# Expert stage: scores of a choice between the sums of v, and at most four gathers in flight

## The chip, the core and the metric

The kernel runs on one core of a Trainium2 chip, as one program. The metric is the device time of one execution in microseconds. Three runs of the kernel before took 4378.47 us in the median (4372.89 to 4390.06). A further execution was taken by the hardware profiler; all rows below are of that one.

## The reference, cut to what matters

The network has two blocks; the first has two layers, each with a product-key expert part, `_peer`. For a token, eight heads each choose 16 of 16384 experts; an expert is one row of `u` and one row of `v`, of 1024 numbers each.

```python
def _peer(h, wq, keys, u, v):
    """PEER: 8 product-key retrieval heads over N_KEYS^2 single-neuron experts. h (B,S,D)."""
    ...
    def block(hb):
        tc = hb.shape[0]
        q = (hb @ wq).reshape(tc, PEER_HEADS, 2, PEER_HALF)
        s = jnp.einsum('thpk,hpnk->thpn', q, keys)
        s_top, i_top = lax.top_k(s, PEER_TOPK)
        cand = s_top[:, :, 0, :, None] + s_top[:, :, 1, None, :]
        cid = i_top[:, :, 0, :, None] * N_KEYS + i_top[:, :, 1, None, :]
        best, pos = lax.top_k(cand.reshape(tc, PEER_HEADS, -1), PEER_TOPK)
        eid = jnp.take_along_axis(cid.reshape(tc, PEER_HEADS, -1), pos, -1)
        g = jax.nn.softmax(best.astype(jnp.float32), -1).astype(hb.dtype)
        act = jax.nn.gelu(jnp.einsum('td,thed->the', hb, u[eid]), approximate=False)
        return jnp.einsum('the,thed->td', g * act, v[eid])
```

The first layer does this for 512 tokens (256 of the context, 256 of the sequence), the second for 256. Everything is float32.

## The kernel before, in words

The program is a chain of stages with a barrier between them. The change is in `stage_peer`, which runs twice: `l0_peer_experts` with four tiles of 128 tokens and `l1_peer_experts` with two. A step is one tile and one head: 32 steps in the first run, 16 in the second. Within a run the engines work as a pipeline over steps, and each engine has its own fixed program:

- TensorE (`pe`): `score(step)` multiplies the queries with the keys (L1195). Then, for each of the 16 experts of the step before (`step = b - 1`), it multiplies the gathered rows of `v` with a diagonal matrix of weights and adds them into the PSUM tile `acc` (L1217); that is called the sum of v here. A sum posts the semaphore `added`.
- VectorE (`dve`): for each expert of step `b` the dot product of the gathered row of `u` with the token (L1361), which posts `dotted`. After dot k of step b comes piece k of `pick(b + 2, k)`, the choice of the experts two steps on: piece 0 (L1270) waits for the scores, the pieces are linked by the semaphore `chain`, and the last one (L1326) writes the indices and posts `chosen`. `weigh` (L1342) makes the weights of the step before after dot 1.
- ScalarE (`act`): softmax exponentials (L1227), the gelu of the 16 dot products (L1249), and the 16 diagonal matrices (L1241).
- GpSimd (`pool`): one indirect DMA for each expert of `u` (L1182) and of `v` (L1187). Each gathers 128 rows of 4 KB, 0.52 MB. The rows of `u` land in eight slots of the weight buffer, those of `v` in eight slots of `ring`, and each slot has a semaphore of its own, `landed[...]`. In step b the gathers alternate: u of (b, k), then v of (b - 1, k). A gather of u waits for the dot that frees its slot (`dotted`, eight experts back), a gather of v for the sum that frees its slot (`added`, eight experts back). Nothing else limits how many are under way.

The order on each engine is the order in which this code is written; there is no scheduler. A score for step b + 2 stands in TensorE's order ahead of all 16 sums of step b - 1, and behind all sums of step b - 2.

Of the kernel before, what the change touches and what calls it, by code (L numbers as in the profile page):

```python
# [52 lines left out]
@contextmanager  # L53
def stage(nc, name):

    with ExitStack() as ctx:
        st = Stage(nc, name, ctx)
        yield st
        for s in st.sems:
            nc.gpsimd.sem_clear(s)  # L60
        nc.all_engine_barrier()
# [1060 lines left out]
HEADS, TOPK, KEYS = 8, 16, 128  # L1122
# [4 lines left out]
def stage_peer(nc, name, h, n_tiles, q_t, k_t, u, v, iota, ident, layer, y, diag, slots, landed, landed0):  # L1127

    RING = TOPK // 2
    with stage(nc, name) as st:
        v_ring = st.sb("ring", [P, RING, D])
        u_ring = slots.rearrange("p s k n -> p (s k n)").rearrange("p (s d) -> p s d", d=D)
# [24 lines left out]
        dotted, added, scored, chosen, h_ready, gelu_done, soft_in, soft_out, w_ready, diag_ready, sum_taken, chain = (  # L1159
            st.sem(n) for n in names)  # L1160
        steps = n_tiles * HEADS

        def landing(step, k):

            return landed0 + 16 * (2 * step + k // RING + 1)

# [3 lines left out]
        with nc.Block() as block:  # L1170
            @block.gpsimd
            def _(pool):
                for b in range(steps + 1):
                    if b < steps:

                        pool.wait_ge(chosen, b + 1)
                    for k in range(TOPK):
                        if b < steps:
                            if b * TOPK + k >= RING:

                                pool.wait_ge(dotted, b * TOPK + k - RING + 1)
                            pool.indirect_dma_start(u_ring[:, k % RING, :], None, u, bass.IndirectOffsetOnAxis(ap=picks[:, b % 4, k:k + 1], axis=0)).then_inc(landed[k % RING], 16)  # L1182
                        if b:
                            if (b - 1) * TOPK + k >= RING:

                                pool.wait_ge(added, (b - 1) * TOPK + k - RING + 1)
                            pool.indirect_dma_start(v_ring[:, k % RING, :], None, v, bass.IndirectOffsetOnAxis(ap=picks[:, (b - 1) % 4, k:k + 1], axis=0)).then_inc(landed[RING + k % RING], 16)  # L1187

            @block.tensor
            def _(pe):  # L1190
                def score(step):

                    t, head = divmod(step, HEADS)
                    for i in range(2):
                        last = nc.tensor.matmul(sc[:, step % 2, i, :], q_t[:, t, 2 * head + i, :], k_t[:, 2 * head + i, :], start=True, stop=True)  # L1195
                    last.then_inc(scored, 1)

                score(0)
                score(1)
                for b in range(steps + 1):  # L1200
                    if b + 2 < steps:

                        pe.wait_ge(chosen, b + 1)
                        score(b + 2)
                    if not b:
                        continue
                    step = b - 1
                    t, head = divmod(step, HEADS)
                    if head == 0 and t:

                        pe.wait_ge(sum_taken, t)
                    for k in range(TOPK):

                        pe.wait_ge(landed[RING + k % RING], landing(step, k))
                        pe.wait_ge(diag_ready, step * TOPK + k + 1)
                        for c in range(2):
                            last = nc.tensor.matmul(acc[:, c * BANK:(c + 1) * BANK], diag[:, step % 2 * TOPK + k, :], v_ring[:, k % RING, c * BANK:(c + 1) * BANK],  # L1217
                                                    start=(head == 0 and k == 0), stop=(head == HEADS - 1 and k == TOPK - 1))
                        last.then_inc(added, 1)
# [966 lines left out]
def peer(nc, weights, name, layer, n_tiles, consts, a, keys_t, h, h_t, y, landed, landed0):  # L2186

    with ExitStack() as ctx:
        sb = buffers(nc, ctx)
        q_t = sb(f"{name}_q_t", [P, n_tiles, HALVES, P])  # L2190
        stage_linear(nc, f"{name}_q", weights, h_t, token_tiles(n_tiles), q_t, feature=True)
        stage_peer(nc, f"{name}_experts", h, n_tiles, q_t[:, :, :, :], keys_t[:, :, :], a["peer_u"].rearrange("l e d -> (l e) d"),
                   a["peer_v"].rearrange("l e d -> (l e) d"), consts["iota"][:, :], consts["ident"][:, :], layer, y,
                   h_t[:, :, :].rearrange("p c (i t) -> p (c i) t", t=P), weights.slots[:, :, :, :], landed, landed0)
# [245 lines left out]
```

## Time and profile before

| what | value |
|---|---|
| median of three runs | 4378.47 us |
| profiled execution | 4386.04 us, its span 4384.2 us |
| busy: PE, DVE, POOL, ACT | 3239.2, 1863.4, 1443.9, 694.2 us |
| gathers: u, v | 768 and 768, 0.94 us of POOL each |
| data moved by the software queue | 805.40 MB of 1028.15 MB |

Read it so. The engines' busy times are of the whole span; the expert stages are the stretches from 785 to 2275 us and from 2795 to 3541 us, in which the line of the DMA is at 9 and the rate above 350 GB/s. POOL works there only. A row of the timeline has the start, the duration, the engine, the line and the tiles, and in brackets how long the engine sat idle before it and what ended that. "remote" and "issue" name no releaser of this program, and a wait that ended with many semaphore updates at once can be put down to any of them.

### The profile page before, as it was taken

The page shows a single profiled execution, that of the slowest core. Times are in us where ns is not written, and L with a number is a line of the kernel's source. Part 1 is how long each engine was busy: PE and PEld are TensorE (multiplying, and loading weights), DVE is VectorE, ACT ScalarE, POOL GpSimd, SP SyncE. Part 2 cuts the span into 40 slices and gives each one's busy share as a digit, 9 for nine tenths or more (in the row PEclk, how much of TensorE's full clock was granted, in tenths as well). Part 3 has the DMA queues.
Part 4 walks back from the last instruction along what each step waited for, and adds up shares of the span by engine and source line. Part 5 has one row for each costly group of instructions (what it writes and reads, how often), then busy time and mean ns, then how long its engine had stood idle before and what let it go on. Part 6 is the DMA issues. An engine that isn't in the chain of part 4 may idle for free. (4 is left out here: it accounts for less than half of the span.)

```text
span 4384.2 us, 28129 instructions
## 1 busy us (share of the span) xinstructions
PE 3239.2 (74%) x8452; PEld 1526.8 (35%) x8452; DVE 1863.4 (43%) x4661; ACT 694.2 (16%) x1660; POOL 1443.9 (33%) x1540
## 2 busy tenths in 40 slices
PE   6888769476767676776766886577677768888888
PEld 2343334222322232222223343422222234634573
DVE  1024630755556565555533073565556423232200
ACT  0012310111211111112110121112112113021100
POOL 0000000566666666666640000366666610000000
PEclk8987879799888898988888887788888989998999
DMA  4123221799989999999981233599999954332333
GB/s 170 66 80 113 80 86 38 295 366 351 375 350 357 364 362 354 371 361 359 370 323 63 79 116 115 212 359 366 355 354 372 362 195 144 112 115 99 115 132 125
DMA packets 355218, 1028.15 MB, mean 235 GB/s; under 512 B 53492, under 2 KB 58100, under 8 KB 355060
## 3 DMA queue, kind: packets, MB, share of 16 engines
q0 software_dynamic: 221184, 805.40, 47.8%
q1 hardware_dynamic: 131824, 217.57, 14.6%
q10 hardware_dynamic: 2068, 3.47, 0.3%
q8 instruction: 66, 1.08, 0.1%
q14 instruction: 76, 0.62, 0.0%
HBM read 1025.19 MB, written 1.15 MB: 234 GB/s over the span
## 5 line engine op out<-in xcount | busy, mean ns | idle before, releaser
L1217 PE MATMUL l_peer_experts_acc<-l_peer_experts_ring,h_t 128*128 128x512 f32 x3072 | 1541.5, 649 | 666.3 <-ACT h_t L1241 261.4
L1182 POOL DMA_INDIRECT weight_slots<-in_peer_u,l_peer_experts_picks x768 | 721.9, 940 | 1552.4 <-DVE l_peer_experts_picks L1326 1309.7
L1217 PEld LDWEIGHTS l_peer_experts_acc<-l_peer_experts_ring,h_t 128*128 128x128 f32 x3072 | 595.8, 204 | 1584.9 <-issue 1104.2
L1361 DVE SCALAR_TENSOR_TENSOR weight_slots<-weight_slots,l_peer_experts_h 128x1024 f32<-128x1024 f32 x768 | 933.1, 1215 | 462.3 <-DMA weight_slots<-in_peer_u,l_peer_experts_picks 371.6
L1187 POOL DMA_INDIRECT l_peer_experts_ring<-in_peer_v,l_peer_experts_picks x768 | 721.8, 940 | 539.0 <-PE l_peer_experts_acc L1217 220.9
L1241 ACT ACTIVATE h_t<-const_ident,l_peer_experts_wgt 128x128 f32<-128x128 f32 x768 | 229.5, 387 | 412.0 <-issue 236.1
L190 PE MATMUL l_peer_q_acc<-h_t,weight_slots 128*128 128x512 f32 (+1 forms) x512 | 171.2, 498 | 5.3 <-DVEq L282 5.3
L190 PEld LDWEIGHTS l_peer_q_acc<-h_t,weight_slots 128*128 128x128 f32 x512 | 100.2, 196 | 75.9 <-issue 62.5
L190 PE MATMUL b_mlp_acc<-weight_slots,b_up 128*128 128x512 f32 x256 | 113.1, 605 | 12.1 <-DVEq L282 12.1
L1227 ACT ACTIVATE l_peer_experts_soft<-l_peer_experts_best,l_peer_experts_low 128x16 f32<-128x16 f32 x48 | 14.8, 307 | 671.5 <-DVE l_peer_experts_low L1305 363.8
L1270 DVE MAX8 l_peer_experts_top<-l_peer_experts_scores 128x8 f32<-128x128 f32 x48 | 14.3, 299 | 242.5 <-remote 157.7
L190 PE MATMUL b_mlp_acc<-b_h_t,weight_slots 128*128 128x256 f32 x512 | 112.5, 383 | 2.2 <-ACTq L268 2.2
L1249 ACT ACTIVATE l_peer_experts_gel<-l_peer_experts_dots 128x16 f32<-128x16 f32 x48 | 10.3, 216 | 625.2 <-issue 554.1
L190 PEld LDWEIGHTS b_mlp_acc<-b_h_t,weight_slots 128*128 128x128 f32 x512 | 98.3, 192 | 16.2 <-ACTq L268 2.5
L190 PE MATMUL b_g_acc<-weight_slots,b_h_t 128*128 128x512 f32 x192 | 88.1, 613 | 10.8 <-ACTq L268 10.8
L209 DVE COPY l_peer_q_t<-l_peer_q_acc 128x512 f32 (+1 forms) x16 | 8.2, 553 | 174.8 <-PE l_peer_q_acc L190 174.8
L190 PEld LDWEIGHTS b_mlp_acc<-weight_slots,b_up 128*128 128x128 f32 x256 | 49.6, 194 | 75.1 <-issue 75.1
L616 PE MATMUL l_ln_turned<-const_ident,h_tiles 128*128 128x128 f32 x80 | 18.8, 413 | 75.2 <-DVE h_tiles L595 75.2
L1361 DVE DVE_READ_ACCUMULATOR weight_slots<-weight_slots,l_peer_experts_h 128x1 f32 x768 | 63.6, 83 | 1.7 <-issue 1.5
L1227 ACT ACT_TABLE_LOAD x44 | 56.5, 1283 | 48.8 <-issue 48.4
L190 PE MATMUL ab_qk_acc<-h_t,weight_slots 128*128 128x512 f32 x128 | 57.1, 609 | 5.3 <-DVEq L282 5.3
L1195 PE MATMUL l_peer_experts_scores<-l_keys_t,l_peer_q_t 128*128 128x128 f32 x192 | 31.9, 294 | 38.1 <-DVE l_peer_experts_picks L1326 33.7
(424 smaller groups left out, 3295.0 us busy)
## 6 DMA issues: line engine op xcount, KB each, us to landing
weight_slots<-in_w_mod SPq DMA_DIRECT2D x24, 2048.0 KB, 8.0
weight_slots<-in_w_in SPq DMA_DIRECT2D x20, 2048.0 KB, 7.9
weight_slots<-in_peer_wq SPq DMA_DIRECT2D x8, 2048.0 KB, 8.1
weight_slots<-in_w_mlp_up SPq DMA_DIRECT2D x8, 2048.0 KB, 7.9
weight_slots<-in_w_mlp_down SPq DMA_DIRECT2D x8, 2048.0 KB, 7.8
weight_slots<-in_peer_u,l_peer_experts_picks POOLq DMA_INDIRECT x768
l_peer_experts_ring<-in_peer_v,l_peer_experts_picks POOLq DMA_INDIRECT x768
weight_slots<-in_gla_w_in SPq DMA_DIRECT2D x6, 2048.0 KB, 8.1
```

The source lines that it names most:

```text
L190: last = nc.tensor.matmul(acc[0:rows, half, bank, col:col + cols], lhs, rhs, start=(b == 0 and k == 0), stop=(b == kb - 1 and k == KC - 1))
L209: ins = nc.vector.tensor_copy(dst, src)
L616: last = nc.tensor.transpose(ps[:, i % 4, k, :], src, ident)
L1182: pool.indirect_dma_start(u_ring[:, k % RING, :], None, u, bass.IndirectOffsetOnAxis(ap=picks[:, b % 4, k:k + 1], axis=0)).then_inc(landed ...
L1187: pool.indirect_dma_start(v_ring[:, k % RING, :], None, v, bass.IndirectOffsetOnAxis(ap=picks[:, (b - 1) % 4, k:k + 1], axis=0)).then_inc( ...
L1195: last = nc.tensor.matmul(sc[:, step % 2, i, :], q_t[:, t, 2 * head + i, :], k_t[:, 2 * head + i, :], start=True, stop=True)
L1217: last = nc.tensor.matmul(acc[:, c * BANK:(c + 1) * BANK], diag[:, step % 2 * TOPK + k, :], v_ring[:, k % RING, c * BANK:(c + 1) * BANK], ...
L1227: nc.scalar.activation(soft[:, p, :], best[:, :], ACT.Exp, bias=low[:, p:p + 1], accum_out=tot[:, p:p + 1]).then_inc(soft_out, 1)
L1241: nc.scalar.activation(diag[:, step % 2 * TOPK + k, :], ident, ACT.Copy, scale=wgt[:, step % 2, k:k + 1]).then_inc(diag_ready, 1)
L1249: nc.scalar.activation(gel[:, b % 2, :], dots[:, b % 2, :], ACT.Gelu).then_inc(gelu_done, 1)
L1270: nc.vector.max(top[:, 0, 0:8], s[:, 0, :])
L1361: nc.vector.scalar_tensor_tensor(row, row, 1.0, hp[:, :], ALU.mult, ALU.mult, accum_out=dots[:, b % 2, k:k + 1]).then_inc(dotted, 1)
```

## The change

Two edits, both in `stage_peer`. In TensorE's program the score of a step is computed between sum 7 and sum 8 of a step's 16 sums, and one step earlier: in iteration b it is the score of step b + 3, behind a wait for `chosen` of b + 2. Scores 0 to 3 come before the first sum. In GpSimd's program every gather gets a second wait: for the landing of the gather issued four before it (`FLIGHT = 4`, two of u and two of v while both alternate, four of the same kind in the first and the last iteration).

```diff
     RING = TOPK // 2
+    FLIGHT = 4
...
             @block.gpsimd
             def _(pool):
+                def landed_u(step, k):
+
+                    if k < 0:
+                        step, k = step - 1, k + TOPK
+                    if step >= 0:
+                        pool.wait_ge(landed[k % RING], landing(step, k))
+
+                def landed_v(step, k):
+                    if k < 0:
+                        step, k = step - 1, k + TOPK
+                    if step >= 0:
+                        pool.wait_ge(landed[RING + k % RING], landing(step, k))
+
                 for b in range(steps + 1):
+
+                    back = FLIGHT // 2 if 0 < b < steps else FLIGHT
                     if b < steps:
 
                         pool.wait_ge(chosen, b + 1)
@@ -1179,11 +1195,13 @@
                             if b * TOPK + k >= RING:
 
                                 pool.wait_ge(dotted, b * TOPK + k - RING + 1)
+                            landed_u(b, k - back)
                             pool.indirect_dma_start(u_ring[:, k % RING, :], None, u, bass.IndirectOffsetOnAxis(ap=picks[:, b % 4, k:k + 1], axis=0)).then_inc(landed[k % RING], 16)
                         if b:
                             if (b - 1) * TOPK + k >= RING:
 
                                 pool.wait_ge(added, (b - 1) * TOPK + k - RING + 1)
+                            landed_v(b - 1, k - back)
                             pool.indirect_dma_start(v_ring[:, k % RING, :], None, v, bass.IndirectOffsetOnAxis(ap=picks[:, (b - 1) % 4, k:k + 1], axis=0)).then_inc(landed[RING + k % RING], 16)
 
             @block.tensor
@@ -1197,12 +1215,13 @@
 
                 score(0)
                 score(1)
+
+                pe.wait_ge(chosen, 1)
+                score(2)
                 for b in range(steps + 1):
-                    if b + 2 < steps:
-
-                        pe.wait_ge(chosen, b + 1)
-                        score(b + 2)
                     if not b:
+                        pe.wait_ge(chosen, 2)
+                        score(3)
                         continue
                     step = b - 1
                     t, head = divmod(step, HEADS)
@@ -1210,6 +1229,10 @@
 
                         pe.wait_ge(sum_taken, t)
                     for k in range(TOPK):
+                        if k == RING and b + 3 < steps:
+
+                            pe.wait_ge(chosen, b + 2)
+                            score(b + 3)
 
                         pe.wait_ge(landed[RING + k % RING], landing(step, k))
                         pe.wait_ge(diag_ready, step * TOPK + k + 1)
```

GpSimd's queue in the middle of the first expert stage, where u and v alternate; before, a gather waits for the slot's last reader alone:

```order
L1187 DMA l_peer_experts_ring<-in_peer_v,l_peer_experts_picks 128x1024 [waits l0_peer_experts_added]
L1182 DMA weight_slots<-in_peer_u,l_peer_experts_picks 128x1024 [waits l0_peer_experts_dotted]
L1187 DMA l_peer_experts_ring<-in_peer_v,l_peer_experts_picks 128x1024 [waits l0_peer_experts_added]
L1182 DMA weight_slots<-in_peer_u,l_peer_experts_picks 128x1024 [waits l0_peer_experts_dotted,l0_peer_experts_chosen]
L1187 DMA l_peer_experts_ring<-in_peer_v,l_peer_experts_picks 128x1024 [waits l0_peer_experts_added]
L1182 DMA weight_slots<-in_peer_u,l_peer_experts_picks 128x1024 [waits l0_peer_experts_dotted]
```

Now, at the same place of the queue (L1199 and L1205 are the two gathers, `row_landed0` to 7 the slots of u, 8 to 15 those of v):

```order
L1199 DMA weight_slots<-in_peer_u,l_peer_experts_picks 128x1024 [waits row_landed7,l0_peer_experts_dotted]
L1205 DMA l_peer_experts_ring<-in_peer_v,l_peer_experts_picks 128x1024 [waits row_landed15,l0_peer_experts_added]
L1199 DMA weight_slots<-in_peer_u,l_peer_experts_picks 128x1024 [waits row_landed0,l0_peer_experts_dotted]
L1205 DMA l_peer_experts_ring<-in_peer_v,l_peer_experts_picks 128x1024 [waits row_landed8,l0_peer_experts_added]
L1199 DMA weight_slots<-in_peer_u,l_peer_experts_picks 128x1024 [waits row_landed1,l0_peer_experts_dotted]
L1205 DMA l_peer_experts_ring<-in_peer_v,l_peer_experts_picks 128x1024 [waits row_landed9,l0_peer_experts_added]
```

The order of the gathers is the same; each has one wait more, for a landing. TensorE's queue at the beginning of an expert stage, before (L1195 is a score, L1217 a sum; two rows of the first are one score and 32 of the second the 16 sums of a step):

```order
L1195 MATMUL l_peer_experts_scores<-l_keys_t,l_peer_q_t 128x128 x8
L1217 MATMUL l_peer_experts_acc<-l_peer_experts_ring,h_t 128x512 x32
L1195 MATMUL l_peer_experts_scores<-l_keys_t,l_peer_q_t 128x128 x2
L1217 MATMUL l_peer_experts_acc<-l_peer_experts_ring,h_t 128x512 x32
L1195 MATMUL l_peer_experts_scores<-l_keys_t,l_peer_q_t 128x128 x2
```

Now (L1213 is a score, L1240 a sum):

```order
L1213 MATMUL l_peer_experts_scores<-l_keys_t,l_peer_q_t 128x128 x8
L1240 MATMUL l_peer_experts_acc<-l_peer_experts_ring,h_t 128x512 x16
L1213 MATMUL l_peer_experts_scores<-l_keys_t,l_peer_q_t 128x128 x2
L1240 MATMUL l_peer_experts_acc<-l_peer_experts_ring,h_t 128x512 x32
L1213 MATMUL l_peer_experts_scores<-l_keys_t,l_peer_q_t 128x128 x2
```

The fifth score, of step 4, stood behind the 16 sums of step 0 and stands behind eight of them now, and so on in every step: each score is issued half a step of sums earlier.

## Rows read from the trace of the kernel before

**Rows 1.** The page's part 2: DMA's share in 40 slices, and its rate.

```profile
DMA  4123221799989999999981233599999954332333
GB/s 170 66 80 113 80 86 38 295 366 351 375 350 357 364 362 354 371 361 359 370 323 63 79 116 115 212 359 366 355 354 372 362 195 144 112 115 99 115 132 125
```

**Rows 2.** The two expert stages by engine: busy us (count), PEclk, DMA share, GB/s.

```profile
785.00:2275.00 1490.00, 1041.07 (x2154) 415.12 (x2155) 853.45 (x2238) 254.17 (x671) 962.52 (x1024) 0.88 0.94 361
2795.00:3541.00 746.00, 511.45 (x1067) 204.25 (x1068) 423.07 (x1102) 122.65 (x331) 481.18 (x512) 0.88 0.94 360
```

**Rows 3.** Timeline of POOL: first and last gather of each expert stage.

```profile
785.59 1.08 POOL L1182 DMA_INDIRECT weight_slots<-in_peer_u,l_peer_experts_picks  x1 [785.13 <-DVE l_peer_experts_picks L1326]
...
2270.30 0.94 POOL L1187 DMA_INDIRECT l_peer_experts_ring<-in_peer_v,l_peer_experts_picks  x1 [1.89 <-PE l_peer_experts_acc L1217]
...
2795.77 0.94 POOL L1182 DMA_INDIRECT weight_slots<-in_peer_u,l_peer_experts_picks  x1 [524.53 <-DVE l_peer_experts_picks L1326]
...
3534.63 0.94 POOL L1187 DMA_INDIRECT l_peer_experts_ring<-in_peer_v,l_peer_experts_picks  x1 [0.30 <-issue]
```

**Rows 4.** The page's part 5, the two gathers: busy, mean ns, idle before.

```profile
L1182 POOL DMA_INDIRECT weight_slots<-in_peer_u,l_peer_experts_picks x768 | 721.9, 940 | 1552.4 <-DVE l_peer_experts_picks L1326 1309.7
...
L1187 POOL DMA_INDIRECT l_peer_experts_ring<-in_peer_v,l_peer_experts_picks x768 | 721.8, 940 | 539.0 <-PE l_peer_experts_acc L1217 220.9
```

**Rows 5.** Timeline of POOL, about one of its stops.

```profile
1290.34 0.94 POOL L1182 DMA_INDIRECT weight_slots<-in_peer_u,l_peer_experts_picks  x1 [0.30 <-issue]
1291.59 0.94 POOL L1187 DMA_INDIRECT l_peer_experts_ring<-in_peer_v,l_peer_experts_picks  x1 [0.30 <-issue]
...
1310.26 0.94 POOL L1182 DMA_INDIRECT weight_slots<-in_peer_u,l_peer_experts_picks  x1 [0.30 <-issue]
1315.94 0.94 POOL L1187 DMA_INDIRECT l_peer_experts_ring<-in_peer_v,l_peer_experts_picks  x1 [4.74 <-PE l_peer_experts_acc L1217]
1317.18 0.94 POOL L1182 DMA_INDIRECT weight_slots<-in_peer_u,l_peer_experts_picks  x1 [0.30 <-issue]
```

**Rows 6.** Timeline of PE: two sums of v before that stop, one behind.

```profile
1297.91 1.98 PE L1217 MATMUL l_peer_experts_acc<-l_peer_experts_ring,h_t 128*128 128x512 f32 x4 [0.52 <-DMA l_peer_experts_ring<-in_peer_v,l_peer_experts_picks]
1300.42 1.98 PE L1217 MATMUL l_peer_experts_acc<-l_peer_experts_ring,h_t 128*128 128x512 f32 x4 [0.53 <-DMA l_peer_experts_ring<-in_peer_v,l_peer_experts_picks]
...
1320.25 1.12 PE L1217 MATMUL l_peer_experts_acc<-l_peer_experts_ring,h_t 128*128 128x512 f32 x2 [2.33 <-DMA l_peer_experts_ring<-in_peer_v,l_peer_experts_picks]
```

**Rows 7.** A score, line L1195 in 1228 to 1252 us: durations, first and last start.

```profile
L1195 PE MATMUL l_peer_experts_scores<-l_keys_t,l_peer_q_t x4: 272/275/275, 1231.3 to 1231.6; 128*128 128x128 f32 x4
```

**Rows 8.** Timeline of DVE about the piece of the choice that reads it.

```profile
1231.85 0.08 DVE L1361 DVE_READ_ACCUMULATOR weight_slots<-weight_slots,l_peer_experts_h 128x1 f32 x1
1249.50 0.30 DVE L1270 MAX8 l_peer_experts_top<-l_peer_experts_scores 128x8 f32<-128x128 f32 x1 [17.56 <-remote]
```

**Rows 9.** Short stretches by engine, columns as in Rows 2.

```profile
1233.00:1244.00 11.00, 0.00 (x0) 0.00 (x0) 0.00 (x0) 0.00 (x0) 8.18 (x10) 0.64 1.03 420
1250.00:1256.00 6.00, 4.21 (x5) 1.85 (x6) 5.93 (x20) 4.76 (x16) 0.19 (x1) 0.50 0.02 5
1258.00:1266.00 8.00, 8.00 (x20) 3.61 (x19) 7.46 (x23) 1.07 (x3) 5.88 (x7) 1.00 0.91 315
1317.00:1326.00 9.00, 5.01 (x9) 1.62 (x8) 6.38 (x12) 0.42 (x1) 6.69 (x8) 0.74 0.87 274
```

**Rows 10.** The stop of POOL behind that long wait of DVE.

```profile
1255.81 0.94 POOL L1187 DMA_INDIRECT l_peer_experts_ring<-in_peer_v,l_peer_experts_picks  x1 [10.93 <-PE l_peer_experts_acc L1217]
```

**Rows 11.** Line L1270 over the span: what ended DVE's idle time before it.

```profile
  remote: 157.7, 16
  DMA attn_mod_bias<-in_b_mod: 64.7, 6
  issue: 10.8, 4
  PE l_peer_experts_scores L1195: 9.2, 10
```

**Rows 12.** Timeline of DVE: two dots that waited for their gather to land.

```profile
1296.65 1.22 DVE L1361 SCALAR_TENSOR_TENSOR weight_slots<-weight_slots,l_peer_experts_h 128x1024 f32<-128x1024 f32 x1 [0.66 <-DMA weight_slots<-in_peer_u,l_peer_experts_picks]
...
1322.55 1.22 DVE L1361 SCALAR_TENSOR_TENSOR weight_slots<-weight_slots,l_peer_experts_h 128x1024 f32<-128x1024 f32 x1 [1.01 <-DMA weight_slots<-in_peer_u,l_peer_experts_picks]
```

## The prediction, as it was written before the changed kernel ran

> **What bounds the kernel now.** I looked first at DMA's line in the page's part 2. The two stretches at 9 are the expert stages; elsewhere DMA is at 1 to 5, and the change touches nothing there [rows 1]. The table by stage gives 1490 and 746 us for them, 2236 of the profiled 4386.04. In them PE is busy 1041 of 1490 us, DVE 853, POOL 963, and DMA has a share of 0.94 at 361 GB/s, so at first sight DMA is the wall [rows 2]. But a short stretch inside shows 420 GB/s, with POOL back to back and all other engines idle [rows 9]. So 361 is a mean of 420 and of holes.
>
> The pace of the stage is that of the gathers. From first to last they take 2270.30 − 785.59 = 1484.71 us for 1024, and 3534.63 − 2795.77 = 738.86 us for 512: 2223.6 us for 1534 intervals, 1.450 us each [rows 3]. Where POOL is not held, one gather follows the other after 0.94 + 0.30 = 1.245 us (1290.34 to 1291.59), which is 0.524 MB / 1.245 = 421 GB/s, the rate of such a full stretch [rows 5, 9]. At 1.245 us the intervals would add up to 1909.8, so the holes cost 2223.6 − 1909.8 = 313.8 us. POOL's idle time says the same: before v 539.0 − 768 × 0.30 = 309 us, and before u 1552.4 less the two starts (785.1 and 524.5) less 230 = 12 us [rows 3, 4]. Nearly all holes stand before a gather of v.
>
> What is the hole? The row names a sum of v. One such gather starts at 1315.94 after 4.74 us of idle time. It needs the slot of the v gather eight back, which was issued at 1291.59. A gather is seen 6.3 us after its issue (issue 1290.34, dot 1296.65), so that one landed near 1297.9, where PE has a sum of 1.98 us; even the next sum was over at 1302.4 [rows 5, 6, 12]. POOL got the word 13 us later. The same with scores: PE did them at 1231.3 to 1231.9, DVE's piece that waits for them began at 1249.50, after 17.56 us of idle time [rows 7, 8], and by then DMA had gone from 420 to 5 GB/s [rows 9]. I read this so: while DMA runs at 420 GB/s the engines' semaphore posts come late, and they come in when the traffic stops. PE's posts are hit (`added`, `scored`), and POOL stops when its eight v slots are used up. That is an inference; the rows show work finished long before the wait for it ended.
>
> **The change part by part.** *The scores.* PE issues the same matmuls, 4 of 275 ns a score [rows 7], 1.1 us in the middle of a step in place of its start; PE is busy 70% of the stage, so that is free [rows 2]. `chosen` of b + 2 is posted at the end of DVE's iteration b − 1, ahead of the weights without which the sums of b − 1 don't start, so the new wait holds nothing. A score gets half a step more, 16 gathers or 23 us at 1.45, which covers the 17.56 us above. DVE's idle time before L1270, 157.7 + 64.7 + 10.8 + 9.2 = 242 us [rows 11], goes. Little of it is on the path: it delays the dots, the weights and so the first sum of a step, and reaches POOL only where it is longest, as in the stop of 10.93 us in place of 4.74 [rows 5, 10]. I bound this edit by 0 and by seven such differences (one per tile and one over), 7 × 6.2 = 43 us, and take 5 beside the other edit, which removes the late posts themselves if it works.
>
> *The limit.* A gather may start only when the fourth last has landed. Queued behind the waiting gather on POOL are only the other gathers; sums and dots wait for these. Now six gathers' time passes from issue to use: 6.3 / 1.245 = 5.1 under way. The fourth last was issued 4.98 us ago, so each gather would wait 1.3 us at first; but then the queue in front of DMA gets shorter, and the time to landing with it. With four under way the interval is a quarter of the time from issue to landing. Its ends by rows: a gather that starts into an empty queue is used after 1320.25 − 1315.94 = 4.31 us, the next one after 1322.55 − 1317.18 = 5.37, one in the full queue after 6.31 [rows 5, 6, 12]. A quarter of these is 1.08 (below POOL's own 1.245, which then rules), 1.34 and 1.58. A worse sign: in the first 8 or 9 us after a stop, with POOL back to back, DMA moves only 315 and 274 GB/s, 1.66 and 1.91 us a gather, so a short queue is served less well [rows 9]. Three others in flight are nearest to the row of 5.37 with a little more in front; I take 1.39 us, which is 5.56 us to landing and 377 GB/s, 90% of the 420. At that pace I expect the posts to come in time, for in the slow stretches DVE and PE work without holes [rows 9], and the stops of 4.7 us to go.
>
> The sum: 1534 × (1.450 − 1.39) = 92 us, and 5 for the scores: 97. The profiled execution took 4386.04, so 4289; the median of the runs is 7.6 below it: 4281 us.
>
> The Trainium skill bears on this in "DMA: Bandwidth & Descriptors", section "Anatomy of one DMA — SWDGE (gpsimd) path": a DMA costs about 2.0 us plus its bytes over 436e3 per us. For 0.524 MB that is an estimate of 3.2 us, a quarter of which is 0.8: by that rule the limit would never bind and the interval be POOL's 1.245. The trace shows 4.31 us for a gather alone, so the measurement decides, and the margin is thinner than by the page.
>
> **The rivals.** *The limit costs nothing and the posts come.* If the time to landing falls below 4 × 1.27, POOL's pace rules: 1.26 to 1.29 us, 1534 × 0.175 = 268 us less, 4110. For it: 4.31 us alone. Against: 5.37 already with one other in front. Also, at 1.25 DMA is as full as now, and then the posts should be as late as now.
>
> *Slower: the time to landing rules.* If four in flight keep DMA in the state of the first microseconds after a stop, the interval settles where a quarter of 6.1 to 6.3 us puts it, 1.52 to 1.58, and each landing adds its own way to POOL. Then the holes are gone but 1534 × 0.11 = 169 us are added: 4547. It decides from 1.46 us on, that is from 5.83 us between issue and landing. For it: 6.31, 315 and 274 GB/s. Against: those latencies hold queueing that the limit takes away.
>
> *The one pays for the other.* Either the interval comes out at 1.43 to 1.46, or DMA is full for long enough that stops remain, shorter and with waits for landings between: 4360 to 4395, about 4375.
>
> *DMA is at its limit on average.* If what counts were the mean of 361 GB/s, no order of issue would help, and only the 5 us of the scores are left: 4373. The skill has such a rule: in "DMA: Bandwidth & Descriptors", section "Bandwidth", it puts HBM's limit per core at about 358 GB/s. The trace has 420 over 11 us [rows 9], so I give it little.
>
> **How the numbers follow.** My forecast (1.33 to 1.43 us, 4190 to 4345) has a chance of 0.44; the free limit 0.10; latency rules 0.27; the one pays for the other 0.15; DMA's mean 0.04. A measurement of this kernel tells 0.5%, 22 us, from no change. Forecast and free limit are faster but for 0.01 of the edge; the middle cases give 0.03 faster, 0.12 same, 0.04 slower; latency is slower: 0.56 faster, 0.13 same, 0.31 slower. The range runs from 1.29 us (4130) to 1.51 us (4470); outside are half of the free limit and the worse half of the slow case. The likeliest case's own range is 4190 to 4345.
>
> **What would show it.** Right: POOL's idle time before both gathers is spread evenly, some 0.4 to 0.5 us each, ended by DMA landings; no idle time over 4 us before v; DVE's idle time before its L1270 (the scores' reader) under 20 us in all; DMA's share flat near 0.95 and about 375 GB/s through a stage; issue to dot 5.4 to 5.7 us; the stages near 1430 and 712 us. The slow case shows issue to dot over 5.9 and under 350 GB/s. Stops of 4 us that remain before v, with sums long finished, would show that four in flight do not relieve the posts, and my inference on these would be wrong if DMA ran at over 410 GB/s with no stops at all. Scores are wrong if PE waits for `chosen` in the middle of its sums.

## The result, and the profile after

The changed kernel took 4656.8 us in the median of four runs (4654.39 to 4661.5), the kernel before 4381.74 beside it: ratio 1.063, 95% interval 1.0606 to 1.0654, slower. The forecast was 4281, with a range from 4130 to 4470. In each comparison further down, the kernel before took either 4358 to 4408 us or 4109 to 4132 in all its runs, and one chip (that of e9 to e11 and of e18) gave both, so each kernel is compared with the runs of before beside it; I call the first kind a comparison with stops and the second one without.

The page's part 2 after, DMA's share and rate in 40 slices:

```profile
DMA  5132213999999999999993223499999984332343
GB/s 176 46 109 98 97 52 109 323 322 321 327 319 317 319 327 323 324 316 324 316 319 118 92 84 134 168 326 321 322 320 324 318 294 128 107 109 95 124 143 117
```

The two expert stages and a short stretch by engine, columns as in [rows 2]:

```profile
785.00:2465.00 1680.00, 1099.49 (x2164) 413.37 (x2164) 860.17 (x2202) 254.77 (x670) 954.27 (x1019) 0.91 0.91 319
2985.00:3830.00 845.00, 547.71 (x1076) 205.38 (x1076) 421.77 (x1065) 124.53 (x331) 473.75 (x506) 0.90 0.90 317
...
1317.00:1326.00 9.00, 4.82 (x11) 1.67 (x11) 5.00 (x9) 0.00 (x0) 4.68 (x5) 1.00 0.92 329
```

The rate is now flat, without the 420 and the 5 of [rows 9], but its level is 319 GB/s in place of a mean of 361 [rows 2]. Timeline of POOL, first and last gather of each stage, as [rows 3]:

```profile
778.18 1.07 POOL L1199 DMA_INDIRECT weight_slots<-in_peer_u,l_peer_experts_picks  x1 [777.72 <-DVE l_peer_experts_picks L1349]
...
2451.53 0.94 POOL L1205 DMA_INDIRECT l_peer_experts_ring<-in_peer_v,l_peer_experts_picks  x1 [0.31 <-issue]
...
2977.05 0.94 POOL L1199 DMA_INDIRECT weight_slots<-in_peer_u,l_peer_experts_picks  x1 [524.58 <-DVE l_peer_experts_picks L1349]
...
3814.45 0.94 POOL L1205 DMA_INDIRECT l_peer_experts_ring<-in_peer_v,l_peer_experts_picks  x1 [0.34 <-PE l_peer_experts_acc L1240]
```

The gathers take 1673.4 and 837.4 us in place of 1484.7 and 738.9, together 287 more: 1.637 us an interval for 1.450. Everything outside them is 12 us shorter, which makes the 275.5 us between the profiled 4386.04 and 4661.50. POOL's lines of the two gathers, as [rows 4]:

```profile
L1205 POOL DMA_INDIRECT l_peer_experts_ring<-in_peer_v,l_peer_experts_picks x768 | 719.2, 937 | 526.9 <-issue 247.0 <-DMA l_peer_experts_ring<-in_peer_v,l_peer_experts_picks 242.5 <-PE l_peer_experts_acc L1240 33.8
L1199 POOL DMA_INDIRECT weight_slots<-in_peer_u,l_peer_experts_picks x768 | 719.2, 936 | 1849.6 <-DVE l_peer_experts_picks L1349 1302.3 <-DMA weight_slots<-in_peer_u,l_peer_experts_picks 348.9 <-issue 185.6
```

Before v the idle time is 527 us as before (539), yet it is other time: no longer stops of 4.7 us, but shorter waits: 242.5 us of it ended by a landing, 247.0 with no releaser that the trace names. Before u it is 1849.6 − 777.7 − 524.6 = 547 us, where it was 243. Both kinds together wait 0.70 us a gather. DVE's idle time before the reader of the scores, 242.5 us in [rows 11], is 3.9:

```profile
L1293 DVE MAX8 l_peer_experts_top<-l_peer_experts_scores x48: 289/294/300, 768.8 to 3636.9; 128x8 f32<-128x128 f32 x48
its engine sat idle before it (us, times) until:
  PE l_peer_experts_scores L1213: 3.9, 2
```

Now the timeline where the loss is made. POOL, and below it DVE's dots, in the same microseconds:

```profile
1307.97 0.94 POOL L1199 DMA_INDIRECT weight_slots<-in_peer_u,l_peer_experts_picks  x1 [0.30 <-issue]
1310.14 0.94 POOL L1205 DMA_INDIRECT l_peer_experts_ring<-in_peer_v,l_peer_experts_picks  x1 [1.24 <-DMA l_peer_experts_ring<-in_peer_v,l_peer_experts_picks]
1312.10 0.94 POOL L1199 DMA_INDIRECT weight_slots<-in_peer_u,l_peer_experts_picks  x1 [1.02 <-DMA weight_slots<-in_peer_u,l_peer_experts_picks]
...
1318.26 0.94 POOL L1199 DMA_INDIRECT weight_slots<-in_peer_u,l_peer_experts_picks  x1 [1.27 <-DMA weight_slots<-in_peer_u,l_peer_experts_picks]
```

```profile
1311.36 1.22 DVE L1384 SCALAR_TENSOR_TENSOR weight_slots<-weight_slots,l_peer_experts_h 128x1024 f32<-128x1024 f32 x1 [2.56 <-DMA weight_slots<-in_peer_u,l_peer_experts_picks]
...
1317.52 1.22 DVE L1384 SCALAR_TENSOR_TENSOR weight_slots<-weight_slots,l_peer_experts_h 128x1024 f32<-128x1024 f32 x1 [2.05 <-DMA weight_slots<-in_peer_u,l_peer_experts_picks]
```

A dot and the gather two of its kind later wait for the same landing. The dot starts at 1311.36 and 1317.52, POOL's gather at 1312.10 and 1318.26: 0.74 us later, both times with POOL idle. My forecast closed the loop at the dot's start.

### The profile page after: what moved, and what is told of

The parts are those of the page before. It is cut to its first block and busy times, and to the rows that moved or that the text cites. A ratio compares the mean times of both kernels' runs of the same rounds, so it can differ in the third digit from the quotient of the medians.

```text
span 4659.7 us, 29587 instructions
## 1 busy us (share of the span) xinstructions
PE 3319.7 (71%) x8452; PEld 1520.8 (33%) x8452; DVE 1883.9 (40%) x4661; ACT 693.6 (15%) x1660; POOL 1438.7 (31%) x1540
## 3 DMA queue, kind: packets, MB, share of 16 engines
q8 instruction: 66, 1.08, 0.1%
## 5 line engine op out<-in xcount | busy, mean ns | idle before, releaser
L1240 PE MATMUL l_peer_experts_acc<-l_peer_experts_ring,h_t 128*128 128x512 f32 x3072 | 1627.0, 668 | 865.5 <-DMA l_peer_experts_ring<-in_peer_v,l_peer_experts_picks 596.7
L1199 POOL DMA_INDIRECT weight_slots<-in_peer_u,l_peer_experts_picks x768 | 719.2, 936 | 1849.6 <-DVE l_peer_experts_picks L1349 1302.3
L1240 PEld LDWEIGHTS l_peer_experts_acc<-l_peer_experts_ring,h_t 128*128 128x128 f32 x3072 | 592.5, 208 | 1872.6 <-DMA l_peer_experts_ring<-in_peer_v,l_peer_experts_picks 1035.2
L1205 POOL DMA_INDIRECT l_peer_experts_ring<-in_peer_v,l_peer_experts_picks x768 | 719.2, 937 | 526.9 <-issue 247.0
L190 PE MATMUL b_xbc_acc<-b_h_t,weight_slots 128*128 128x256 f32 x256 | 58.1, 388 | 1.9 <-ACTq L268 1.9
L1213 PE MATMUL l_peer_experts_scores<-l_keys_t,l_peer_q_t 128*128 128x128 f32 x192 | 32.5, 298 | 37.7 <-DVE l_peer_experts_picks L1349 33.3
L415 PE MATMUL gla_mod<-weight_slots,silu_c 128*2 128x512 f32 x128 | 58.8, 614 | 0.0
```

What stands on the lines that cost most here:

```text
L190: last = nc.tensor.matmul(acc[0:rows, half, bank, col:col + cols], lhs, rhs, start=(b == 0 and k == 0), stop=(b == kb - 1 and k == KC - 1))
L415: ins = self.nc.tensor.matmul(self.banks[i % len(self.banks)][0:2, :], self.silu_c[:, k, :], self.weights.slots[:, slot, k, :], start=(k = ...
```

## The experiments

The expectations name the explanations by letters: A, each gather waits for a landing, and that loop sets the pace; B, DMA itself delivers less with few gathers in flight; C, the scores at their new place cost the time; D and E, the stops come with the depth of DMA's queue or with its rate; F, the added wait instruction costs POOL time by itself.

**Which half of the change costs the time.** `e1_scores_alone` drops the landing waits, `e2_limit_alone` puts the scores back.

```diff
-                            landed_u(b, k - back)
-                            landed_v(b - 1, k - back)
```

> The scores at their new place, no limit on the gathers. Theory A (the limit costs the time: each gather waits for its fourth last landing, 1.642 us a gather in place of 1.450): the stops of POOL before v remain, DVE's idle time before its reader of the scores falls from 242 us to under 10, and the time is 4340 to 4380 us. Rival C (the scores in the middle of the sums cost the time): above 4600 us.

> The limit of four, the scores at their old place. Theory A: 4640 to 4675 us, as the changed kernel, since in it no semaphore post comes late and the scores are not waited for at either place. Rival C: under 4400 us.

This comparison was without stops: before took 4119.39 us. Scores alone 4114.41, ratio 0.9995 (0.9975 to 1.0015); limit alone 4667.07, 1.1317 (1.1289 to 1.1346). So the limit carries all of the loss (rival C falls), and my "the stops remain" for the first was a miss for an unforeseen reason: there were none to remain. The stage of e1, a short stretch of it, and POOL's v gathers:

```profile
785.00:2090.00 1305.00, 1020.49 (x2156) 394.04 (x2157) 862.38 (x2214) 254.15 (x671) 956.57 (x1021) 0.95 1.01 411
1233.00:1244.00 11.00, 10.34 (x27) 4.27 (x25) 6.72 (x18) 1.68 (x3) 8.25 (x10) 1.00 1.02 418
```

```profile
L1203 POOL DMA_INDIRECT l_peer_experts_ring<-in_peer_v,l_peer_experts_picks x768 | 719.5, 937 | 269.8 <-issue 198.3 <-PE l_peer_experts_acc L1238 70.9 <-DVE weight_slots L1382 0.6
```

DMA runs at 418 GB/s with PE and DVE at work beside it, where [rows 9] had 420 with both idle: at that rate the posts of PE and DVE can come in time. The interval is 1.271 us. The landings do come late, as part 6 of the page has it, the median from issue to landing of the gathers of u, in e1 and then in the changed kernel (e8):

```profile
weight_slots<-in_peer_u,l_peer_experts_picks POOLq DMA_INDIRECT x768, 12.9
...
weight_slots<-in_peer_u,l_peer_experts_picks POOLq DMA_INDIRECT x768, 5.7
```

A landing is 16 posts to its semaphore. In e1 the fifteenth comes 8.1 us after the issue on average and the last one 12.5 us, in e8 5.4 and 5.7 us. A dot of e1 starts 12.6 us after its gather. POOL does not stop for that, as a slot may be in use for 16 gathers, 20 us at this pace.

**Is it DMA, or the way from a landing to the next gather?** A gather with two waits is two instructions: the wait that the code names second stands alone, ahead of the gather on which the first rides. `e3_waits_swapped` exchanges them:

```diff
+                            landed_u(b, k - back)
                             if b * TOPK + k >= RING:
 
                                 pool.wait_ge(dotted, b * TOPK + k - RING + 1)
-                            landed_u(b, k - back)
```

> The changed kernel with the two waits of each gather in the other order of code: the landing of the fourth last first, then the slot's reader. The first wait rides on the gather itself, the other is an instruction of its own ahead of it; now the landing rides on the gather. Theory A (the loop from landing to next gather rules, and 0.737 us of it lie between the separate wait instruction and the gather's start, while a wait that rides on the gather is followed by its start in about 0.12): the loop of 6.57 us gets 0.6 shorter, the interval 0.15, so 1.49 us and 4657 - 1534 x 0.15 = 4427 us. Rival B (with four in flight DMA delivers 319 GB/s, whenever they are issued): earlier issue only lengthens the time to landing, 4650 to 4660 us.

4550.76 us, ratio 1.1046 (1.1025 to 1.1067) beside 1.1317 of the limit alone: 116 us less by order alone. Its POOL, and its dots:

```profile
1306.59 0.94 POOL L1199 DMA_INDIRECT weight_slots<-in_peer_u,l_peer_experts_picks  x1 [0.50 <-PE l_peer_experts_acc L1240]
...
1315.91 0.94 POOL L1199 DMA_INDIRECT weight_slots<-in_peer_u,l_peer_experts_picks  x1 [1.15 <-DMA weight_slots<-in_peer_u,l_peer_experts_picks]
```

```profile
1306.36 1.22 DVE L1384 SCALAR_TENSOR_TENSOR weight_slots<-weight_slots,l_peer_experts_h 128x1024 f32<-128x1024 f32 x1 [1.33 <-DMA weight_slots<-in_peer_u,l_peer_experts_picks]
...
1315.68 1.22 DVE L1384 SCALAR_TENSOR_TENSOR weight_slots<-weight_slots,l_peer_experts_h 128x1024 f32<-128x1024 f32 x1 [1.48 <-DMA weight_slots<-in_peer_u,l_peer_experts_picks]
```

The gather follows the dot by 0.23 us, no longer 0.74. Half of the 230 us that theory A promised came, for two reasons. "Landing" here and in the table below is the end of the last of a gather's 16 semaphore packets, the packets taken in order of time. Over gathers 40 to 999, the mean from the fourth last landing to a gather's start fell from 1.30 to 0.84 us, and the mean from issue to landing rose from 5.24 to 5.37: the sum went from 6.54 to 6.21, a quarter of it from 1.64 to 1.55. So the way got 0.46 us shorter and not 0.6, and B is right for a quarter of that, 0.13, which DMA's queue took back. The semaphores' records say the same more sharply: where POOL stood on a landing, its gather starts 0.76 us after the last post in the changed kernel (e2 and e8 too) and 0.26 us after it in e3, in the median. The expectation had taken 0.12 for the latter.

**Does the loop predict other limits?** `e4_flight6` and `e11_flight8` change the number, `e6_flight5_swapped` and `e7_flight6_swapped` are five and six with the waits exchanged, `e5_flight5` and `e10_flight3` (and e6) wait for a landing of the other kind while u and v alternate; the edit of e5:

```diff
-                            landed_u(b, k - back)
+                            if 0 < b:
+                                landed_v(b - 1, k - 3)
+                            else:
+                                landed_u(b, k - FLIGHT)
...
-                            landed_v(b - 1, k - back)
+                            if b < steps:
+                                landed_u(b, k - 2)
+                            else:
+                                landed_v(b - 1, k - FLIGHT)
```

> The changed kernel with a limit of six. Theory A: a gather in a full queue takes 6.0 to 6.3 us to land, with 1.14 from landing to start 7.2 to 7.4, over 6 is 1.21 to 1.24, below POOL's own 1.245: the limit hardly binds. Then either the stops return, as DMA is again at 420 GB/s (4340 to 4380 us, as with the scores alone), or, if it was the depth of the queue and not the rate that made the posts late, no stops are left: 1.26 us a gather and 4657 - 1534 x 0.38 = 4074 us. Rival B expects 4074 to 4380 as well, and is not told apart here.

> The changed kernel with a limit of five: a gather waits for the landing of the fifth last, which while u and v alternate is one of the other kind. Theory A (loop: interval = (issue to landing + landing to start) / limit): with four in front a gather takes 5.66 us to land, as in the run with a limit of six, and from landing to start 1.14, with 0.1 for uneven landings 6.9; over 5 is 1.38 us, so 4657 - 1534 x 0.26 = 4255 us. Rival B (what counts is the rate that DMA reaches, and the time to landing gives way): with a rate between those of four (319 GB/s) and six (408 GB/s) in flight the same direction but halfway, 4400 us.

> A limit of five and the waits in the other order, the landing's riding on the gather. With four in flight that took 0.43 us off the way from landing to start and gave 0.14 back to landing. Theory A: 6.9 - 0.3 = 6.6, over 5 is 1.32 us, 4657 - 1534 x 0.32 = 4166 us. Rival B: no gain over the limit of five without it.

> A limit of six and the waits in the other order. Theory A: the loop is 6.6 to 6.9 us, over 6 is 1.10 to 1.15, under POOL's own 1.245, so the limit binds only after a disturbance: 1.25 to 1.27 us, 4115 to 4140 us. Where the kernel before runs at 4119 us there is nothing to gain and 4115 to 4140 is expected; where it runs at 4378, with the stops, theory D (the stops come with the depth of the queue) says 4140 and theory E (they come with the rate, 420 GB/s) says 4300 to 4400.

> The changed kernel itself beside the kernel before on one chip. In the first comparison before took 4378 us; beside the four experiments it took 4119, without its stops, on another chip. If the loop rules the changed kernel, its time doesn't depend on that: 4645 to 4675 us, and the ratio is 1.063 or 1.13 as before takes 4378 or 4119.

> The changed kernel with a limit of three. Theory A (loop): issue to landing with two in front 4.95 us, landing to start 1.14, 0.1 for uneven landings, 6.2 over 3 is 2.07 us; 4657 + 1534 x (2.07 - 1.64) = 5317 us, 254 GB/s in the expert stages. Rival B (DMA's rate at a short queue is a matter of its own): the rate of four in flight is 319; in proportion three give 239 GB/s or 2.19 us, 5500 us.

| run | limit | us (before beside it) | interval | issue to landing | landing to start | issue to last post |
|---|---|---|---|---|---|---|
| e10 | 3 | 5184.13 (4386.13) | 1.965 | 4.74 | 1.16 | 5.06 (60 gathers) |
| changed, first | 4 | 4656.80 (4381.74) | 1.637 | 5.24 | 1.30 | – (records merged) |
| e8, changed | 4 | 4664.87 (4116.24) | 1.636 | 5.21 | 1.32 | 5.67 |
| e3, exchanged | 4 | 4550.76 (4119.39) | 1.556 | 5.37 | 0.84 | 5.86 |
| e5 | 5 | 4240.64 (4116.24) | 1.359 | 5.37 | 1.42 | 5.88 |
| e6, exchanged | 5 | 4171.16 (4116.24) | 1.312 | 5.43 | 1.08 | 6.03 |
| e4 | 6 | 4146.02 (4119.39) | 1.290 | 5.74 | 1.95 | 6.65 |
| e7, exchanged | 6 | 4132.01 (4116.24) | 1.276 | 5.78 | 1.82 | 6.75 |
| e1, none | – | 4114.41 (4119.39) | 1.271 | 7.25 | – | 12.52 |

(Means over gathers 40 to 999; the interval is from all 1534.) The last column goes by the landing semaphore's own records. The two columns before it go by packets in order of time. A post follows its packet by about 0.35 us (4.11 and 4.44 us for the first gather of e8), and where one of the 16 parts lags behind the others the order of time counts a landing too early besides, by about 5 us in e1. Landing and start add up to limit times interval in any run, by what they are, so that this sum fits is no test. The tests are the order of e3 and the times forecast: theory A said 4255 and 4166 for e5 and e6, and 4240.64 and 4171.16 came. e4 met neither of its numbers, 4074 without stops and 4340 to 4380 with them: its interval was 1.290 and not 1.26. e8 repeats the changed kernel at ratio 1.1333 (1.1313 to 1.1353): its time doesn't depend on the kind of comparison, only that of before does. e10 came 130 us under theory A's 5317, since I took 4.95 us to landing and it is 4.74; B's 5500 is further off. The stages at three, five and six:

```profile
805.00:2820.00 2015.00, 1205.26 (x2164) 438.11 (x2165) 867.35 (x2238) 254.12 (x671) 961.73 (x1024) 0.86 0.82 267
```

```profile
785.00:2190.00 1405.00, 1051.80 (x2164) 402.76 (x2164) 863.10 (x2217) 254.72 (x672) 955.98 (x1022) 0.93 0.99 382
```

```profile
785.00:2105.00 1320.00, 1026.41 (x2147) 398.76 (x2148) 860.96 (x2209) 254.19 (x671) 954.90 (x1020) 0.94 1.01 406
```

At six the loop hardly binds (POOL stands idle for over 0.35 us before 92 gathers, at four before 952), and a gather only takes longer to land.

**Where the time of before differs, and whether a limit removes the stops.**

> The kernel before, profiled on a chip of the experiments, where it took 4116 to 4119 us and not 4378. If the 260 us between lie in POOL's stops (313.8 us over the pace of 1.245 us were counted in the first profile), POOL's idle time before the gathers of v is 230 to 280 us in place of 539, the first expert stage's gathers take about 1300 us in place of 1485, and DMA is at 415 to 420 GB/s throughout. If they lie elsewhere (other stages, the clock), the idle time before v stays above 450 us.

> The changed kernel with a limit of eight: a landing wait that hardly ever binds, so that what is left is the price of one more wait instruction in front of each gather. Theory A: POOL's pace stays 1.245 us (its 0.737 us from the wait instruction to the gather's start fit beside the 0.5 us after the gather before), and the time is that of the kernel before on the same chip within 0.5%. Rival F (each wait instruction costs POOL 0.1 us or more): 1534 x 0.1 = 150 us slower or more.

This comparison fell on one with stops, so e9 shows the kernel before as it was (4408.01 us) and my expectation of it went unmet for that reason. Its v gathers, which answer to [rows 4], and beside them those of the limit of six in a comparison with stops (e12):

```profile
L1187 POOL DMA_INDIRECT l_peer_experts_ring<-in_peer_v,l_peer_experts_picks x768 | 719.4, 937 | 535.1 <-issue 211.7 <-PE l_peer_experts_acc L1217 194.3 <-remote 77.6
```

```profile
L1205 POOL DMA_INDIRECT l_peer_experts_ring<-in_peer_v,l_peer_experts_picks x768 | 719.3, 937 | 501.0 <-issue 209.5 <-PE l_peer_experts_acc L1240 177.2 <-remote 62.5
```

Against 269.8 us in e1, that is 265 us of stops. The profile of e9 is 297 us longer than that of e1 (4408.01 and 4110.61): 265 of it lies in the stretches of the gathers, and the rest nearly all ahead of the first one. Of the 275 us between the first profile of before and e1, 273 lie in them. So the stops are nearly all of the difference between the two kinds of comparison. The kernel before was never profiled in a comparison without stops; e1 stands for it here. e11 took 4348.62, ratio 0.9914 (0.9886 to 0.9942): one more wait instruction per gather costs POOL next to nothing (rival F falls; 1.423 us a gather, against 1.420 in e14 without it). It came 37 us faster where I had expected no change within 0.5%; that is the worth of the scores, as e14 shows. The next four ran in another comparison with stops (before 4382.77):

> A limit of six once more. On a chip without stops 4146 us, as before. On a chip with stops (before at 4378 to 4386): theory D (depth of the queue makes the posts late; at most six are under way instead of up to seven or more) 4140 to 4170 us; theory E (the rate does; six in flight run at 408 GB/s, above the 377 at which I expected the posts in time) 4300 to 4390 us.

> A limit of five with the landing's wait riding on the gather, 401 GB/s where there are no stops, 4171 us there. On a chip with stops: theory D 4171 us; theory E, whose threshold lies somewhere between 319 and 420 GB/s, 4171 to 4350 us.

> The scores alone. On a chip without stops the time of before within 0.3%. On a chip with stops 4345 us (-38, as a limit of eight, if that hardly binds and its gain belongs to the scores; 5 to 43 us was the forecast) or 4380 (if the gain belongs to the limit of eight).

> The changed kernel without any landing wait; instead GpSimd writes a small spare tile ahead of each gather of v, which slows its pace. If that takes x us, POOL's interval is 1.245 + x / 2 on average, and nothing else changes: with x of 0.1 to 0.3 us, 1.30 to 1.40 us and 390 to 405 GB/s, 4116 + 1534 x 0.05 to 0.15 = 4190 to 4350 us on a chip without stops. On a chip with stops: theory E (rate) the same 4190 to 4350, without stops; theory D (depth) the same too, so only stops that remain at this rate speak against E.

e12, six: 4340.00, ratio 0.9894 (0.9861 to 0.9927). e13, five with the waits exchanged: 4359.75, 0.9957 (0.9934 to 0.9980). e14, scores alone: 4347.87, 0.9937 (0.9905 to 0.9970). e15: 4350.89, 0.9917 (0.9890 to 0.9945). The stops stay: 74, 53, 68 and 67 gathers start over 3 us after the one ahead, 75 in the first profile of before, and 20 in the changed kernel. Theory D (depth) falls for depths from five on, as five and six in flight have stops too; theory E's numbers came (e13's but for 10 us), but the rate it blames was there in e1 without a stop. The scores bring 35 us here and nothing in e1's comparison; e11 and e12 hold them too and gain little beyond them. e15 told nothing of the pace: its 64 numbers hid in POOL's own 0.30 us.

The last three asked for the pace of the forecast. In e17 GpSimd writes a spare tile ahead of each gather, and nothing waits for a landing:

```diff
+                def spend():
+                    if count[0]:
+                        pool.wait_ge(paced, count[0])
+                    nc.gpsimd.memset(spare[:, :], 0.0).then_inc(paced, 1)
+                    count[0] += 1
```

> A limit of five once more; 1.36 us a gather and 4241 us where there are no stops. On a chip with stops: theory E (the rate makes the posts late, and 385 GB/s is low enough, as I forecast for 377) 4241 to 4260 us, gathers over 3 us late only every 98; if 385 GB/s is still too much, or it is not the rate, stops remain and the time is 4300 to 4420 us.

> No landing wait; GpSimd writes 192 numbers of a spare tile ahead of each gather of u and of v. 64 numbers took 0.170 us and made the pace 1.26 us; 1.1 ns a number more gives 0.93 + 0.31 + 0.16 = 1.40 us between gathers, 375 GB/s. Without stops 4117 + 1534 x 0.14 = 4335 us on any chip. On a chip with stops: theory E, 4335 us, none left and DVE and PE never late; if stops remain at this pace, 4400 us or more.

> The limit of five a third time. On a chip without stops 4235 to 4245 us. On a chip with stops: theory E with a threshold above 385 GB/s 4241 to 4260 us and gathers over 3 us late only every 98; if stops remain, 4300 to 4420 us.

All three fell on comparisons without stops (before 4114.26 and 4114.03): e16 4238.06, ratio 1.0319 (1.0283 to 1.0355); e18 4254.36, 1.0336 (1.0319 to 1.0353); e17 4295.30, 1.0438 (1.0420 to 1.0455). They repeat the limit of five and leave the question open. e17 came 40 us under its 4335, since the pace went from 1.271 to 1.386 us and not by 0.14. e17's stage and a piece of its POOL:

```profile
785.00:2210.00 1425.00, 1049.70 (x2164) 401.60 (x2164) 857.44 (x2198) 255.75 (x671) 1237.68 (x2035) 0.94 0.98 376
```

```profile
1300.87 0.28 POOL L1194 MEMSET l_peer_experts_spare<- 128x192 f32 x1
1301.32 0.94 POOL L1207 DMA_INDIRECT weight_slots<-in_peer_u,l_peer_experts_picks  x1 [0.17 <-issue]
1302.27 0.27 POOL L1194 MEMSET l_peer_experts_spare<- 128x192 f32 x1
```

At an even 1.386 us and 376 GB/s no gather is over 3 us late. This is the stage that I had forecast, reached by pace and not by a limit of four; beside a kernel before without stops it is 4% slower, since that one's gathers already follow each other about every 1.27 us (e1).

## Why the prediction was wrong

**The pace under the limit: the step that failed.** I wrote that "with four under way the interval is a quarter of the time from issue to landing", and took 5.56 us. I read it as the time to a dot's start, and that came almost as forecast: 5.24 to landing and a median of 0.40 from there to a dot's start, 5.64. But the loop closes at the next gather's start, and the wait for the landing was an instruction of its own, followed by the gather 0.74 us later. I read "landing" off the starts of dots [rows 12], an engine whose waits ride on its instructions, and closed POOL's loop with it. By terms: (5.64 − 5.56) / 4 × 1534 = 31 us, 0.74 / 4 × 1534 = 284, and 0.16 us that is left, 61: together 376, which is 4657 − 4281. That it comes out to the microsecond is luck, as gains and losses outside the gathers happen to cancel. The 20 gathers over 3 us late hold about 50 of the 61 us. e3 shows that 0.51 of the 0.74 us is the instruction's order and not DMA; exchanging the waits took 116 us off, since DMA took back 0.13 us of it a loop. The other 0.23 us remains with the wait on the gather itself. The missing term could have been looked for: the order after has two waits at each gather, and POOL's 1.245 us from gather to gather can hide work that a late wait lays bare.

**The rival of the slower side** had the sign and the place, a loop of landings, but its price came from the wrong term: it wanted 6.1 to 6.3 us to landing, and gave 4547. It even said that "each landing adds its own way to POOL", and put no price on that way, in its own sum or in the forecast's. The change was dearer although DMA was as quick as hoped.

**The rule for one DMA.** Runs at three, four and five in flight took 4.74, 5.24 and 5.37 us from issue to landing, and all three limits bound. The Trainium skill's "DMA: Bandwidth & Descriptors", section "Anatomy of one DMA — SWDGE (gpsimd) path", gave an estimate of 3.2; the runs decide against it, as the trace of before had.

**The stops.** Half right. They go with the limit of four, also beside a kernel before that has them: the changed kernel's 20 late gathers are not those stops, as 15 of them come every 98 gathers, in e8 too. But the cause that I inferred, the rate of 420 GB/s, is not enough: I had named a run "at over 410 GB/s with no stops at all" as what would refute it, and e1 is that but for four gathers, 3.1 to 3.7 us behind the one ahead. In the traces with stops the records of `dotted` in the first stage number 200 (before) and 192 (e14) for 512 dots, against 513 in e1: updates were merged or late there. It is so for DMA's posts too: a slot of u has 424 records for 1536 posts in before, and 1536 in e1. In the changed kernel's own profile the two numbers are 511 and 1460. What puts a comparison into the one kind or the other is open; it is not the chip. Whether something else used the chip's memory at those times is not on record; DMA itself still reached 420 GB/s between stops [rows 9]. Whether the stops end between about 400 GB/s (the pace of e6; its repeat e13 has 53 of them) and 319 is open too: the limit of five in the first order of waits never met a comparison with stops.

**DMA's mean as a limit.** This rival is refuted: e1 moved 411 GB/s over 1305 us.

**The scores.** Right. DVE's 242 us became 3.9, PE paid nothing for their place, and their worth lay between my bounds of 0 and 43: 35 us with stops (e14), 0 without (e1). With the limit the posts come in time anyway (e2 against e8), as I had said of taking only 5.

**What was to be seen** came out so: issue to dot 5.73 us (5.4 to 5.7 named, 5.9 for the slow case); no idle time over 4 us before v; DVE under 20; but DMA at 319 GB/s and not 375 (the slow case said under 350), 0.70 us of waiting a gather and not 0.4 to 0.5, stages of 1673 and 837 us and not 1430 and 712.

No version beats the kernel before in both kinds of comparison. The scores alone come nearest: 0.9937 with stops, 0.9995 (interval over 1) without.

## What to carry to other kernels

A limit on transfers in flight is a loop, and where it binds its pace is the whole loop over the limit: from issue to landing, from landing to the waiting engine, and from there to the next issue, with all that this engine otherwise prepares while it waits. Where an instruction needs two waits, let the one that ends last ride on it, and look in the order of instructions which does. Measure a suspected stall in more than one session before building on it: all but 5 us of this forecast's 97 us of gain was a stall that the kernel before often does not have.

## What the runs showed of the hardware that I had not expected

- From a separate wait on POOL to the start of the indirect gather behind it pass 0.74 us (median of 1484, from the trace's records); with the landing's wait on the gather itself the gather starts 0.23 us after a dot that waits for the same landing. Counted from the semaphore's last post it is 0.76 and 0.26 us. Unhindered, POOL keeps 1.245 us either way (e11).
- One gather of 0.52 MB: 3.9 to 4.1 us from issue to landing with none in front (the first of a stage), 4.74 with two, 5.24 with three, 5.74 at a limit of six, all by packets. By the semaphore it is 5.7 us at a limit of four, 6.65 at six, and 12.5 at 418 GB/s with no limit, where the last of a landing's 16 posts comes 4.5 us behind the fifteenth.
- At a limit of four to six, every 98th gather of a stage starts 3.4 to 4.6 us after the one ahead, with no releaser: 15 times in the changed kernel, in e5 and in e4. At 2.3 us over POOL's pace that is 35 us, about what the limit of six is above no limit (4146.02 and 4114.41). With the waits exchanged it is 2.4 to 3.9 us (e3, e6, e7), in the mean 2.64 in e7 for 3.60 in e4, and 15 times that difference is the 14 us between their times; at a limit of eight (e11) and with none (e1) most of these gathers start at POOL's pace. The cause is open. One such row of the changed kernel:

```profile
1125.42 0.94 POOL L1205 DMA_INDIRECT l_peer_experts_ring<-in_peer_v,l_peer_experts_picks  x1 [2.94 <-issue]
```

- A write of 64 numbers in each partition ahead of a gather of v costs POOL's pace 0.02 us, one of 192 numbers ahead of every gather 0.14.
